# The value half of an attention compression, moved into the first score units, with another form of its gelu

## The reference, cut to what matters

```
def compress(raw, j):                       # j = 0: keys, j = 1: values
    blk = raw[:, tok] + cmp_pos[j]          # 31 windows of 32 tokens x 64 columns
    hid = gelu(blk @ cmp_w1[j] + cmp_b1[j]) # 2048 -> 256 columns, gelu in its tanh form
    return hid @ cmp_w2[j] + cmp_b2[j]      # 256 -> 64 columns

s_cmp = q @ k_cmp ; p_cmp = masked_softmax(s_cmp) ; o_cmp = p_cmp @ v_cmp
```

## Time and profile before

| | us |
|---|---|
| median of 3 runs (1528.43 to 1529.43) | 1528.6 |
| the profiled execution, its whole time | 1528.77 |
| span of its trace | 1527.1 |
| TensorE matmuls, busy | 1500.8 (98%) |
| VectorE, busy | 1067.8 (70%) |
| ScalarE, busy | 696.5 (46%) |
| GpSimd, busy | 271.9 (18%) |
| the chain of work that ended last: TensorE's share | 95% |

### The profile page before, as it was taken

One profiled execution on the slowest core, in us unless ns is written; L12 is line 12 of the kernel. 1 busy time (PEld: TensorE's weight loads), 2 busy tenths in 40 slices (PEclk: granted clock), 3 DMA queues, 4 the chain that ended last, 5 costly groups with the idle time before them and its releaser, 6 DMA issues.

```text
span 1527.1 us, 20994 instructions
## 1 busy us (share of the span) xinstructions
PE 1500.8 (98%) x8228; PEld 1249.2 (82%) x8228; DVE 1067.8 (70%) x1617; ACT 696.5 (46%) x1206; POOL 271.9 (18%) x205
## 2 busy tenths in 40 slices
PE   6999999999999999989999999999999999999999
PEld 5788888888888897977878888888888898877777
DVE  6798689889988773259885685665635653688665
ACT  4453552322314454347775552332314443777761
POOL 0110013223232000059872011111100011010000
PEclk9999999999999999999999999999999999999999
DMA  9774257478585213330000254344432242111211
GB/s 340 269 263 164 83 212 261 168 250 300 187 285 183 91 53 131 118 116 2 2 2 29 83 193 164 111 153 160 144 108 86 91 162 83 56 55 63 86 74 56
DMA packets 114247, 207.54 MB, mean 136 GB/s; under 512 B 6361, under 2 KB 21990, under 8 KB 114150
## 3 DMA queue, kind: packets, MB, share of 16 engines
q1 hardware_dynamic: 113822, 206.09, 39.3%
q10 hardware_dynamic: 328, 0.12, 0.0%
HBM read 202.00 MB, written 4.19 MB: 135 GB/s over the span
## 4 chain that ended last, share of the span: by engine, by line
PE 95%; DVE 3%; ACT 1%; issue 1%; DMA 1%; SPq 0%; ACTq 0%; DVEq 0%
PE PS L2340 56%; PE PS L2293 20%; PE PS L2694 3%; PE PS L2721 2%; PE PS L2684 2%; PE PS L2501 1%; PE PS L2787 1%; PE PS L2624 1%; PE PS L2364 1%; PE PS L2772 1%; PE PS L2853 1%; PE PS L2875 1%; PE PS L2574 1%; DVE MROW L1448 1%; PE PS L2686 1%
## 5 line engine op out<-in xcount | busy, mean ns | idle before, releaser
L764 ACT ACTIVATE WH<-RAW 128x2048 fp32r<-128x2048 f32 (+1 forms) x102 | 191.2, 1885 | 338.8 <-DMA RAW<-in_ff_w_in_dram 221.2
L1327 DVE TENSOR_TENSOR WL<-RAW,WH 128x2048 fp32r<-128x2048 f32 (+1 forms) x98 | 249.1, 2565 | 73.2 <-ACT WH L764 72.9
L544 POOL PARTITION_ALL_REDUCE MROW<-MACC x25 | 118.5, 4739 | 591.0 <-DVE MACC L1362 504.4
L2340 PE MATMUL PS<-WH,HIDh 128*128 128x512 f32 (+1 forms) x576 | 217.7, 378 | 0.0
L2340 PE MATMUL PS<-WH,HIDl 128*128 128x512 f32 (+1 forms) x576 | 217.5, 378 | 0.0
L2340 PE MATMUL PS<-WL,HIDh 128*128 128x512 f32 (+1 forms) x576 | 217.5, 378 | 0.0
L2340 PE MATMUL PS<-HTh,WH 128*128 128x512 f32 (+1 forms) x520 | 202.6, 390 | 0.0
L2340 PE MATMUL PS<-HTl,WH 128*128 128x512 f32 (+1 forms) x520 | 202.6, 390 | 0.0
L2340 PE MATMUL PS<-HTh,WL 128*128 128x512 f32 (+1 forms) x520 | 202.5, 389 | 0.0
L2340 PEld LDWEIGHTS PS<-WH,HIDh 128*128 128x128 f32 x576 | 108.4, 188 | 20.5 <-issue 0.2
L2340 PEld LDWEIGHTS PS<-WL,HIDh 128*128 128x128 f32 x576 | 108.4, 188 | 20.2
(11 more groups left out here) (380 smaller groups left out, 3065.6 us busy)
## 6 DMA issues: line engine op xcount, KB each, us to landing
MRAW<-in_ada_w_dram SPq DMA_DIRECT2D x40, 1024.0 KB, 7.3
RAW<-in_ff_w_in_dram SPq DMA_DIRECT2D x32, 1024.0 KB, 5.3
RAW<-in_ff_w_out_dram SPq DMA_DIRECT2D x32, 1024.0 KB, 5.1
RAW<-in_w_in_dram SPq DMA_DIRECT2D x16, 1024.0 KB, 5.2
MRAW<-in_w_ada_dram SPq DMA_DIRECT2D x12, 1024.0 KB, 8.7
PIECE<-in_ada_w_dram SPq DMA_DIRECT2D x16, 512.0 KB, 9.8
MRAW<-in_kv_ada_w_dram SPq DMA_DIRECT2D x8, 1024.0 KB, 6.1
RAW<-in_kv_w_dram SPq DMA_DIRECT2D x6, 1024.0 KB, 5.6
```

The costliest lines, as they stand in the source:

```text
L544: pool.partition_all_reduce(MROW[:], acc[:], P, RADD).then_inc(m_red, 1)
L764: act.activation(rounded(u)[:, 0:width(u)], RAW[:, u % 4, 0:width(u)], ACT.Copy).then_inc(w_hi, 1)
L1327: dve.tensor_tensor(WL[:, u % 4, 0:width(u)], RAW[:, u % 4, 0:width(u)], rounded(u)[:, 0:width(u)].bitcast(F32), ALU.subtract).then_inc(w_ ...
L2340: mm = pe.matmul(po, a, b_, start=(k == 0 and i == 0), stop=(k == KT - 1 and i == len(ops) - 1), skip_group_check=len(ops) > 3)
```

## The change

- GpSimd runs an addition of one column (`tensor_tensor`, the same kind of operation as `stage_lo`) after its last `mod()` ahead of the attention and before it waits for the compression's group.
- TensorE makes half of the value rows' first half (8 of 16 matmuls) before the keys' second product, and the other half after it. The second half of the value rows, 16 matmuls, goes into iterations 3 to 7 of the attention's loop, in front of the scores: three, three, three, three and four.
- The gelu of the values leaves ScalarE's gelu table. VectorE forms x and x times (x squared + 1/0.044715) from PSUM (`value_rows`, iteration 9), ScalarE takes an exponential of that (`gelu_exp`, iteration 10), and VectorE adds one, takes the reciprocal and multiplies with x (`value_gelu`, iteration 11). These work on both halves at once, 248 columns.
- ScalarE's one-column exponential, in front of which its table is loaded, stands after the two gelus of the keys.
- The compressed values are made in iteration 14 in place of 3 (in bank 7 in place of 4), their bias is added in iteration 15 in place of 5, and GpSimd copies them after its weights of step 0. TensorE waits for the copy in iteration 18, where `values(0)` now stands (before: the wait in 12, `values(0)` in 16).
- The tiles PB lie in another order in the same memory, and a tile GE of 248 columns is new.

```diff
@@ -35,6 +35,7 @@
 EPS = 1e-6
...
 FLOOR = -1e25
+GELU_CUBE, GELU_RATE = 0.044715, 2.0 * math.sqrt(2.0 / math.pi)
 HEADS, GROUPS, HD = 16, 4, 64
...
 LAM_INIT = 0.8 - 0.6 * math.exp(-0.3 * 0)
@@ -178,7 +179,7 @@
         return t
     QS = scratch("QS", [P, 4, T], F32R)
-    PB = [at(f"PB{i}", [P, 512], F32, o_rb + 2048 * i if i < 4 else o_mraw + 2048 * (i - 4)) for i in range(12)]
+    PB = [at(f"PB{i}", [P, 512], F32, o_mraw + 2048 * i if i < 8 else o_rb + 2048 * (i - 8)) for i in range(12)]
     KCF, HC = scratch("KCF", [P, GROUPS, 32]), scratch("HC", [P, 2, GROUPS * CMP])
...
     B2V = scratch("B2V", [CMP, HD])
@@ -194,6 +195,7 @@
     PT = [scratch(f"PT{i}", [P, 512]) for i in range(6)]
...
     PTC = [scratch(f"PTC{i}", [P, 2 * P]) for i in range(2)]
+    GE = scratch("GE", [P, 2, GROUPS * CMP])
     second = [at(n, [P, 4, T], F32, o) for n, o in (
         ("SQT", o_hid), ("SKT", o_hid + 8192), ("SV", o_hid + 16384), ("SG", o_hid + 24576),
@@ -560,6 +562,7 @@
         for _ in range(18):
             mod()
+        pool.tensor_tensor(SM[:, 47:48], EPST[:], EPST[:], ALU.add)
         pool.wait_ge(full, 4 * group_of["compress"])
...
         pool.memset(MCM[:], 0.0).then_inc(pool_c, 1)
@@ -610,9 +613,6 @@
             for stage in (stage_hi, stage_lo):
...
                     stage(pair, e)
-        pool.wait_ge(kc_r, 3)
-        pool.tensor_copy(VC[32:64, :, HD:2 * HD], VC[0:32, :, 0:HD]).then_inc(vc_copies, 1)
-        pool.wait_ge(vc_copies, 1)
         for S in range(SUPER):
...
             staged = S % 2 == 1 and pair < KT
@@ -622,6 +622,10 @@
                     stage_hi(pair, e)
...
                 weights(PER * S + i)
+            if S == 0:
+                pool.wait_ge(kc_r, 3)
+                pool.tensor_copy(VC[32:64, :, HD:2 * HD], VC[0:32, :, 0:HD]).then_inc(vc_copies, 1)
+                pool.wait_ge(vc_copies, 1)
             if staged:
...
                     stage_lo(pair, e)
@@ -1052,18 +1056,21 @@
         chunk(kv_br(0))
         chunk(kv_br(1), split=False)
-        for j in range(2):
-            for mo in range(2):
-                act.wait_ge(hc_b, 4 * j + 2 * mo + 2)
-                act.activation(HC[:, mo, :].rearrange("p (g c) -> p g c", c=CMP),
-                               hidden(j, mo)[:, 1:129].rearrange("p (g c) -> p g c", c=32)[:, :, 0:CMP],
-                               ACT.Gelu_apprx_tanh, bias=SM[:, 40 + 2 * j + mo:41 + 2 * j + mo]).then_inc(hc_r, 1)
-            if j == 0:
-                act.wait_ge(kc_f, 1)
-                act.wait_ge(pool_c, 8)
-                act.activation(KCF[:, :, 0:CMP], PS[:, 3, 0:GROUPS * CMP].rearrange("p (g c) -> p g c", c=CMP),
-                               ACT.Identity,
-                               bias=C02[:, P + Q_B2:P + Q_B2 + 1]).then_inc(kc_full32, 1)
+        for mo in range(2):
+            act.wait_ge(hc_b, 2 * mo + 2)
+            act.activation(HC[:, mo, :].rearrange("p (g c) -> p g c", c=CMP),
+                           hidden(0, mo)[:, 1:129].rearrange("p (g c) -> p g c", c=32)[:, :, 0:CMP],
+                           ACT.Gelu_apprx_tanh, bias=SM[:, 40 + mo:41 + mo]).then_inc(hc_r, 1)
+        act.activation(SM[:, 44:45], EPST[:], ACT.Exp)
+        act.wait_ge(kc_f, 1)
+        act.wait_ge(pool_c, 8)
+        act.activation(KCF[:, :, 0:CMP], PS[:, 3, 0:GROUPS * CMP].rearrange("p (g c) -> p g c", c=CMP),
+                       ACT.Identity, bias=C02[:, P + Q_B2:P + Q_B2 + 1]).then_inc(kc_full32, 1)
+        def gelu_exp():
+            act.wait_ge(hc_b, 8)
+            act.activation(GE[:], GE[:], ACT.Exp, scale=-GELU_RATE * GELU_CUBE).then_inc(hc_b, 1)
         def exp(u):
@@ -1099,11 +1106,12 @@
             act.activation(both(HIDh, S), PS[:, 6 + S % 2, 0:2 * P].rearrange("p (t c) -> p t c", c=P), ACT.Copy
                            ).then_inc(a_oh, 1)
-        act.activation(SM[:, 44:45], EPST[:], ACT.Exp)
         act.wait_ge(vc_zero, 3)
...
                 copy(t - COPY_LAG)
+            if t == 10:
+                gelu_exp()
             if t < UNITS:
...
             S, at_ = (t - VALUES_LAG - PER) // PER, (t - VALUES_LAG) % PER
@@ -1832,30 +1840,56 @@
         chunk(kv_br(1), split=False)
-        def hidden_bias(j, mo):
-            ps, i = hidden(j, mo), 2 * j + mo
-            dve.wait_ge(hc_f, i + 1)
-            b = SM[:, 40 + i:41 + i]
-            dve.tensor_tensor(b, ps[:, 0:1], C1[:, C_B1 + i:C_B1 + i + 1], ALU.add).then_inc(hc_b, 1)
-            dve.wait_ge(hc_b, 2 * i + 1)
+        def hidden_bias(mo):
+            ps = hidden(0, mo)
+            dve.wait_ge(hc_f, mo + 1)
+            b = SM[:, 40 + mo:41 + mo]
+            dve.tensor_tensor(b, ps[:, 0:1], C1[:, C_B1 + mo:C_B1 + mo + 1], ALU.add).then_inc(hc_b, 1)
+            dve.wait_ge(hc_b, 2 * mo + 1)
             dve.tensor_tensor(b, ps[:, 128:129], b, ALU.add).then_inc(hc_b, 1)
-        hidden_bias(0, 0)
-        hidden_bias(0, 1)
-        hidden_bias(1, 0)
+        def value_rows():
+            dve.wait_ge(hc_f, 4)
+            dve.wait_ge(kc_f, 1)
+            b, v = SM[:, 42:44], HC[:].rearrange("p m (g c) -> p m g c", c=CMP)
+            ps = PS[:, 6:8, 1:129].rearrange("p m (g c) -> p m g c", c=32)[:, :, :, 0:CMP]
+            dve.tensor_tensor(b, PS[:, 6:8, 0], C1[:, C_B1 + 2:C_B1 + 4], ALU.add).then_inc(hc_b, 1)
+            dve.wait_ge(hc_b, 5)
+            dve.tensor_tensor(b, PS[:, 6:8, 128], b, ALU.add).then_inc(hc_b, 1)
+            dve.wait_ge(hc_b, 6)
+            for mo in range(2):
+                last = dve.tensor_scalar(v[:, mo], ps[:, mo], SM[:, 42 + mo:43 + mo], None, ALU.add)
+            last.then_inc(hc_r, 1)
+            dve.wait_ge(hc_r, 3)
+            dve.tensor_tensor(GE[:], HC[:], HC[:], ALU.mult).then_inc(hc_b, 1)
+            dve.wait_ge(hc_b, 7)
+            dve.scalar_tensor_tensor(out=GE[:], in0=GE[:], scalar=1.0 / GELU_CUBE, in1=HC[:],
+                                     op0=ALU.add, op1=ALU.mult).then_inc(hc_b, 1)
+        def value_gelu():
+            dve.wait_ge(hc_b, 9)
+            dve.tensor_scalar(GE[:], GE[:], 1.0, None, ALU.add).then_inc(hc_b, 1)
+            dve.wait_ge(hc_b, 10)
+            dve.reciprocal(GE[:], GE[:]).then_inc(hc_b, 1)
+            dve.wait_ge(hc_b, 11)
+            dve.tensor_tensor(HC[:], HC[:], GE[:], ALU.mult).then_inc(hc_r, 1)
+        hidden_bias(0)
+        hidden_bias(1)
         dve.wait_ge(kc_full32, 1)
...
         dve.tensor_tensor(KCl[:], KCF[:], KCh[:].bitcast(F32), ALU.subtract).then_inc(kc_r, 1)
-        hidden_bias(1, 1)
         def compressed_values():
...
             dve.wait_ge(vc_zero, 3)
-            dve.tensor_tensor(VC[0:CMP, :, 0:HD], PS[0:CMP, 4, 0:GROUPS * HD].rearrange("p (g d) -> p g d", g=GROUPS),
+            dve.tensor_tensor(VC[0:CMP, :, 0:HD], PS[0:CMP, 7, 0:GROUPS * HD].rearrange("p (g d) -> p g d", g=GROUPS),
                               B2V[:, None, :].to_broadcast([CMP, GROUPS, HD]), ALU.add).then_inc(kc_r, 1)
@@ -1942,7 +1976,9 @@
                 copy(t - COPY_LAG)
...
                 negmax(t)
-            if t == 5:
+            if t == 11:
+                value_gelu()
+            elif t == 15:
                 compressed_values()
...
             if (t - 2) % PER == 0 and S < SUPER:
@@ -1957,6 +1993,8 @@
                         weights(PER * S + 4)
...
                     weights(PER * S + 3 * (at_ // 4 + 1))
+            if t == 9:
+                value_rows()
             S = (t - VALUES_LAG - PER - 1) // PER
...
                 out_lo(S)
@@ -2616,20 +2654,21 @@
         chunk("A", HIDh, HIDl, mixed=True)
         chunk("A", HIDh, HIDl, mixed=True)
-        def hidden_rows(j, mo):
+        def hidden_rows(j, mo, first=0, last=16):
             pe.wait_ge((cw0_in, cw1_in[mo])[j], 16)
-            for m in range(16):
+            for m in range(first, last):
                 half = m // 8
...
                                skip_group_check=True)
-            mm.then_inc(hc_f, 1)
+            if last == 16:
+                mm.then_inc(hc_f, 1)
         evicted(35)
...
         hidden_rows(0, 1)
-        hidden_rows(1, 0)
+        hidden_rows(1, 0, last=8)
         pe.wait_ge(hc_r, 2)
...
         pe.wait_ge(ev_a, freed(37)[0])
@@ -2638,14 +2677,14 @@
             mm = pe.matmul(PS[:, 3, 0:GROUPS * CMP], W2K[:, mo].rearrange("p a d -> p (a d)"), HC[:, mo, :],
...
         mm.then_inc(kc_f, 1)
-        hidden_rows(1, 1)
+        hidden_rows(1, 0, first=8)
         def compressed_values():
...
                 for mo in range(2):
-                    mm = pe.matmul(PS[0:CMP, 4, HD * h:HD * h + HD], HC[:, mo, CMP * h:CMP * h + CMP],
+                    mm = pe.matmul(PS[0:CMP, 7, HD * h:HD * h + HD], HC[:, mo, CMP * h:CMP * h + CMP],
                                    W2V[:, mo, :], start=(mo == 0), stop=(mo == 1))
             mm.then_inc(kc_f, 1)
@@ -2724,13 +2763,16 @@
             mm.then_inc(a_pv, 1)
         for t in range(UNITS + VALUES_LAG):
+            if 3 <= t < 8:
```

(8 more changed lines are left out.)

## The result

| | before | after |
|---|---|---|
| median of 15 executions, us | 1528.77 (1527.97 to 1531.45) | 1531.98 (1530.28 to 1534.61) |
| ratio, 95% interval | 1 | 1.002 (1.0012 to 1.0028) |
| the profiled execution: time, span, us | 1528.77, 1527.1 | 1530.28, 1528.6 |

What follows compares the result with a forecast made beforehand. TensorE bounds the kernel, so only its waits count. Scores(15) +2.1, VectorE operations blocked by GpSimd +0.4, TensorE's later idle time -0.5: +2.0 us on the median 1528.6 gives 1530.6 us, whole range 1527.0 to 1532.8.

Steps and rivals of the forecast that it cites:

- signs of being wrong: Product before 662, reciprocal under 0.6 or over 2, negmax(12) before 681, or clock under 1.00 around 664.
- The gate and the start: Keys' second product waits for B2V's landing at 663.3; scores(0) start at 665.60 in place of 667.34, -1.74 us.
- GpSimd's operation and the key split: Early one-column operation hides GpSimd's configuration change; staging done by 662.5, key split from 2.52 to at most 0.90 us.
- Scores(7): Scores(4) to (7) with 13 value matmuls added: scores(7) start near 672.95, -1.4 us against before.
- VectorE: Iterations 9 and 11: value_rows adds 1.75 us, value_gelu 2.4 us with gaps, its reciprocal 1.60 us.
- the rows' slope: Reciprocals of 12 and 32 columns give 5.8 ns a column, so 1.60 us for the 248-column one.
- The port: New VectorE operations on SBUF held up by GpSimd's weights: +0.4 us, range 0 to 3.
- the port rival: Four new VectorE operations each wait on GpSimd's weights, 2.8 us in place of 0.4: 1533.0 us; chance 0.14.
- Scores(15): Reciprocal block delays negmax(12) by 2.1 to 2.2 us; scores(15) go from 681.92 to 684.0, +2.1 us.
- inside that wait: Compressed values in iteration 14, 1.0 us, run from 682.4 to 683.4 while TensorE waits for scores(15).
- The clock: Rival: TensorE's 2.8 us idle, 660.5 to 663.3, drops the grant to 1.2 GHz: 1533.6 us; chance 0.05.
- the recovery: Behind scores(15), TensorE's idle time takes back 0.5 us (range 0 to 1); late weights' transposes have some 3 us spare.

Runs made afterwards that it cites:

- run 5: The kernel before with GpSimd's one-column operation alone added; 1528.81 us, ratio 0.9997 to before.
- Run 9: The changed kernel with ScalarE's tanh and GpSimd's copy behind the casts, without dummy matmuls; 1533.00 us, ratio 1.0025 to before.
- run 3: The changed kernel with dummy matmuls into an unused bank before scores(12) and scores(13); 1531.98 us, ratio 1.0019 to before.
- run 7: The changed kernel with GpSimd's copy of the compressed values moved behind the first casts of the next head pair; 1531.15 us, ratio 1.0018 to before.
- run 1: The changed kernel with the reciprocal of 248 columns left out; 1533.14 us, ratio 1.0025 to before.
- run 2: The changed kernel with ScalarE's tanh for the exponential and one VectorE operation in place of three; 1532.67 us, ratio 1.0024 to before.
- run 4: The changed kernel without GpSimd's one-column operation; 1535.41 us, ratio 1.0041 to before.
- run 6: The changed kernel with ScalarE's tanh and the dummy matmuls together; 1531.30 us, ratio 1.0010 to before.
- run 8: The changed kernel with tanh, dummy matmuls and GpSimd's copy behind the casts; 1529.19 us, ratio 1.0004 to before.
- run 11: The changed kernel with tanh, dummies, copy behind casts, and small transfers issued between the value weight's halves; 1526.88 us, ratio 0.9987 to before.

## Why the prediction came out as it did

The time was in the range and the sign of the sum right. Two of its signs of being wrong, a product before 662 and negmax(12) before 681, are there in plain time (661.37 and 680.33), but not by position: after's first value row itself is 1.1 us earlier. Its steps:

- **The gate and the start.** Right in kind: the product waits for the transfers. In size too small: forecast -1.74 us at scores(0), measured -2.6 behind the first value row. 0.85 us of that is the product itself, at +3.70 us in place of +4.55: SyncE issued `W2V` at -0.6 in place of -0.2 us, and the last small packets ended sooner. Why is not known; run 5, with GpSimd's operation alone, has the product at +4.59, so it is not that.
- **GpSimd's operation and the key split.** Right. The subtraction follows the cast after 0.15 us, and the split took 0.23 + 0.29 us, even less than the 0.90 allowed.
- **Scores(7).** Forecast -1.4, measured -2.3, the same 0.9 as at the start.
- **VectorE.** `value_rows` 1.75 forecast, 1.94 measured with its gaps; `value_gelu` 2.4 and 2.47; the reciprocal 1.60 and 1.70. The Trainium skill, VectorE: DVE Perf Modes, "First, the fixed hardware budget", read as eight cycles a column, would have had about 2.1, an estimate: the measurement lies nearer to the rows' slope. (The prediction says that the sum would be 0.4 higher by it; 2.1 less 1.60 is 0.5.)
- **The port.** The +0.4 was not there, nor the port rival: square 0.42 and addition 0.27 beside GpSimd's weights, product 0.42 just behind them (they end at 679.99). What the rival described met an old operation instead, the scaling of 1.35 us at 694.95, beside GpSimd's subtraction.
- **Scores(15).** Forecast +2.1, measured +1.8 by position. This agreement was partly luck. The step named one path, reciprocal, negmax(12) and exponential(12), and that one came out at +1.3 (negmax(12) at 22.66 us in place of 21.34), since the start was 0.9 earlier than forecast. The other path, TensorE's own work at the low clock, which the step did not have, brought it back to +1.8. It said that the compressed values run "inside that wait"; they end at 682.4 and scores(15) start 0.2 later.
- **The clock** was priced as a rival at the early wait, with 0.05. The profile of after has it at 1.00 there and low behind scores(13), a place the prediction did not name; the argument that waits of 1.14 and 1.19 had left it at 1.00 held for waits 9 us apart and not for two in a row with 1.07 us of matmuls between. Run 9 shows the named place falling as well. The Trainium skill, TensorE: Matmul & The Clock Gate, "What's actually happening", says that how busy TensorE has lately been sets the clock; the windows of after and run 3's dummy matmuls agree with it.
- **The step that failed is the recovery.** The sum took 0.5 back behind scores(15), and let GpSimd's later weights fall in "some 3 us to spare". By position 0.6 was indeed taken back at once (scores(16) are 1.2 late in place of 1.8), but it did not last: 0.75 was lost again up to scores(21), which no run here takes apart, and 0.6 at scores(26), so that from there on the kernel is 2.6 us late, 0.8 more than at scores(15). The 0.6 are not a late weight but a late subtraction: behind the copy and the cast GpSimd's weights started 1.8 us after their coefficients were there (684.98 and 686.74), and the subtraction behind them ran onto VectorE's scaling, which took 1.35 in place of 0.71 us and held up the copy that TensorE waits for. With the copy behind the casts (run 7) that scaling takes 0.48 us, but two small operations of VectorE ahead of it take 0.91 and 1.06 beside the subtraction (0.16 and 0.17 in step 0), and so only 0.3 comes back there.

So +2.0 was forecast and +2.6 (position) to +3.2 (medians) measured. The remaining 0.6 us between the two measures goes with the lower clock of the other executions, but only one of them has a profile: in which stretch they lost it stays open.

## What to carry to other kernels

When cutting the suspected cost changes nothing, look at the next wait in line before giving the theory up: here reciprocal and clock hid each other, each alone worth 0 to 0.4 us at scores(15) and together 1.5. When work moves into another engine's loop, ask of every queue what stands behind the new wait, not only who needs the result, and what the delayed work will run beside. A small transfer queued behind a large one that is not needed yet is cheap to move ahead, and gave 1.6 us by position and 2.3 in the median here.

## What the runs showed of the hardware

- Two waits of 1.13 to 1.14 and 1.48 us, with 1.07 us of matmuls between them (after), came with a fall to 1.2 GHz in all six profiles of kernels that have them and no dummies (after, runs 1, 2, 4, 7 and 9): within the second wait in runs 1 and 9, 0.3 us behind it in after and runs 2 and 7, 1.8 us behind it in run 4. Ten dummy matmuls of 128 columns (20 records) in those waits kept it at 2.4 GHz there in all four profiles that had them (runs 3, 6, 8 and 11). The other executions of run 3 had mean clocks from 1.000 down to 0.997, so it fell in some of them too, in places that no profile shows.
- The clock differs between executions of one kernel by falls in places where nothing was changed: 127 to 131 us is low in before and in runs 1, 4, 5 and 6, and at full speed in after and the rest. The first value row then starts at 658.8 to 659.2 us, without it at 657.2 to 658.2 (659.35 once). Two profiles can thus differ by over 1 us ahead of the code under study.
- A reciprocal of 248 columns took 1.70 us, where other operations of VectorE of that width took 0.27 to 0.47.
- VectorE's operations in SBUF took longer where they ran beside GpSimd's two-tensor subtraction: a scaling of 512 columns 1.35 us (0.48 in run 7, with the subtraction over), operations of 12 columns 0.91 and 1.06 us in run 7 (0.16 and 0.17 in after, with no subtraction running).
